# Causal attention pairs on Trainium2: the softmax normalisation moved from VectorE to ScalarE, and two steps of the transposes exchanged

## The reference, cut to what matters

```python
s = jnp.einsum('bqhd,bkhd->bhqk', q_blk, k) * scale     # (+ cumulative forget terms in FoX)
s = jnp.where(k_pos[None, :] <= q_pos[:, None], s, NEG_INF)
p = jax.nn.softmax(s, axis=-1)
return jnp.einsum('bhqk,bkhd->bqhd', p, v)
```

## Time and profile before

| | us |
|---|---|
| median of 3 runs | 1988.62 |
| the runs | 1988.26, 1993.39, 1988.62 |
| profiled execution | 1987.94 |
| its span, first to last instruction | 1986.1 |

### The profile page before, as it was taken

One profiled execution on the slowest core, in us unless ns is written; L12 is line 12 of the kernel. 1 busy time (PEld: TensorE's weight loads), 2 busy tenths in 40 slices (PEclk: granted clock), 3 DMA queues, 4 the chain that ended last, 5 costly groups with the idle time before them and its releaser, 6 DMA issues.

```text
span 1986.1 us, 23674 instructions
## 1 busy us (share of the span) xinstructions
PE 1797.5 (91%) x9188; PEld 1421.2 (72%) x9188; DVE 842.9 (42%) x1805; ACT 761.6 (38%) x1536; POOL 596.5 (30%) x291
## 2 busy tenths in 40 slices
PE   7998998999899999989998979976878999999978
PEld 6676676787688777766666758765756888788766
DVE  1556626586524544254656362576434111000042
ACT  3445543455234434434455433223334232212241
POOL 4222223321343222333212212322102444444422
PEclk9999998999999999989999987887998999999989
DMA  5211233232442221432111324212112333233311
GB/s 145 59 38 41 64 128 111 65 79 50 150 128 75 62 65 54 138 92 59 42 41 54 114 68 108 64 53 64 43 47 65 93 95 105 85 96 95 111 59 64
DMA packets 215578, 157.19 MB, mean 79 GB/s; under 512 B 54635, under 2 KB 197771, under 8 KB 215468
## 3 DMA queue, kind: packets, MB, share of 16 engines
q1 hardware_dynamic: 205120, 128.37, 23.1%
q10 hardware_dynamic: 10044, 27.03, 4.6%
q0 software_dynamic: 304, 0.29, 0.1%
HBM read 146.49 MB, written 9.04 MB: 78 GB/s over the span
## 4 chain that ended last, share of the span: by engine, by line
PE 61%; DVE 11%; ACT 4%; issue 2%; ACTq 2%; POOL 1%; DMA 1%; POOLq 0%; DVEq 0%
PE banks L457 18%; PE banks L459 17%; PE banks L458 16%; PE banks L645 3%; PE banks L615 2%; PE banks L660 2%; POOL w_lo L2300 1%; DVE AB L1875 1%; PE banks L629 1%; DVE AB L1970 1%; DVE AB L1968 1%; ACT w_hi L1115 1%; ACTq L1601 1%; DVE AB L1961 1%; DVE misc L2177 1%
## 5 line engine op out<-in xcount | busy, mean ns | idle before, releaser
L2300 POOL TENSOR_TENSOR w_lo<-w_raw,w_hi 128x1024 fp32r<-128x1024 f32 (+4 forms) x255 | 584.2, 2297 | 1359.1 <-ACT w_hi L1115 1359.0
L457 PE MATMUL banks<-XTh,w_hi 128*128 128x512 f32 (+2 forms) x1080 | 437.3, 405 | 20.2 <-DVE XTl L1918 6.2
L458 PE MATMUL banks<-XTl,w_hi 128*128 128x512 f32 (+2 forms) x1080 | 428.7, 397 | 0.0
L459 PE MATMUL banks<-XTh,w_lo 128*128 128x512 f32 (+2 forms) x1080 | 427.8, 396 | 0.0
L1115 ACT ACTIVATE w_hi<-w_raw 128x1024 fp32r<-128x1024 f32 (+4 forms) x255 | 253.2, 1002 | 223.2 <-PE banks L459 136.9
L457 PEld LDWEIGHTS banks<-XTh,w_hi 128*128 128x128 f32 (+1 forms) x1080 | 209.1, 194 | 71.4 <-issue 19.9
L458 PEld LDWEIGHTS banks<-XTl,w_hi 128*128 128x128 f32 (+1 forms) x1080 | 209.2, 194 | 43.6 <-issue 1.5
L459 PEld LDWEIGHTS banks<-XTh,w_lo 128*128 128x128 f32 (+1 forms) x1080 | 208.2, 193 | 44.9
L1875 DVE TENSOR_SCALAR AB<-AB,ri 128x256 f32<-128x256 f32 (+3 forms) x256 | 186.4, 791 | 2.3
L457 PE MATMUL banks<-w_hi,OTh 128*128 128x512 f32 (+1 forms) x448 | 171.5, 383 | 9.6 <-POOL w_lo L2300 4.2
L459 PE MATMUL banks<-w_hi,OTl 128*128 128x512 f32 (+1 forms) x448 | 167.9, 375 | 0.0
(11 more groups left out here) (200 smaller groups left out, 2511.7 us busy)
## 6 DMA issues: line engine op xcount, KB each, us to landing
w_raw<-in_w_gate_up_dram SPq DMA_DIRECT2D x44, 512.0 KB, 3.8
w_raw<-in_fox_w_in_dram SPq DMA_DIRECT2D x30, 512.0 KB, 4.0
w_raw<-in_mla_w_in_dram SPq DMA_DIRECT2D x26, 512.0 KB, 4.0
w_raw<-in_w_in_dram SPq DMA_DIRECT2D x24, 512.0 KB, 3.7
w_raw<-in_w_down_dram SPq DMA_DIRECT2D x22, 512.0 KB, 3.5
w_raw<-in_swa_w_in_dram SPq DMA_DIRECT2D x20, 512.0 KB, 3.8
w_raw<-in_mla_w_out_dram SPq DMA_DIRECT2D x16, 512.0 KB, 3.5
x_spill<-AB ACTq DMA_DIRECT2D x12, 512.0 KB, 2.6
```

Of the source, the lines that this page charges most:

```text
L457: nc.tensor.matmul(o, ah, bh, start=first, stop=False, skip_group_check=True)
L458: nc.tensor.matmul(o, ah, bl, start=False, stop=False, skip_group_check=True)
L459: return nc.tensor.matmul(o, al, bh, start=False, stop=last, skip_group_check=True)
L2300: pool.tensor_tensor(view(w_lo, u, RING), view(w_raw, u, RAW), view(w_hi, u, RING).bitcast(F32), ALU.subtract).then_inc(lo_done, 1)
```

## The change

In causal pairs DVE makes only the reciprocals (new semaphore `pinv`) and ACT multiplies the rows; in window pairs DVE goes on multiplying, in a form that also writes an accumulator into an unused tile. PE's steps 4 and 5 are exchanged. In `scores`, the plain products of all tiles of a chunk come first, then the rope or forget ones, and only the first tile's first product has the start flag.

```diff
+                    for t in pr.s_chunks[ch]:
+                        ts, ks, cols = at(t)
                         for n, (qp, kp) in enumerate(((QKh, QKh), (QKh, QKl), (QKl, QKh))):
...
-                                                      start=n == 0, stop=n == 2 and not pr.rope and not pr.aug, skip_group_check=True)
+                                                      start=n == 0 and t == pr.s_chunks[ch][0],
+                                                      stop=n == 2 and not pr.rope and not pr.aug, skip_group_check=True)
+                    for t in pr.s_chunks[ch]:
+                        ts, ks, cols = at(t)
                         if pr.aug:
...
                     elif n == 4:
+                        turn(i, 1, 0)
+                    elif n == 5:
                         scores(i + 2, 1)
-                    elif n == 5:
-                        turn(i, 1, 0)
...
+                def norm(i, x):
+                    if not 0 <= i < n_pairs or pairs[i].window:
+                        return
+                    pr, b = pairs[i], (a0 + i) % 2
+                    c.inv += 1
+                    act.wait_ge(pinv, c.inv)
+                    for t in range(T):
+                        sc = pr.score(b, x, t)
+                        ins = nc.scalar.activation(sc, sc, ACT.Copy, scale=ri[:, b, 4 * x + t:4 * x + t + 1])
+                    ins.then_inc(pnorm, 1)
...
                     exps(i + 1, 1)
+                    norm(i + 1, 0)
                     fill(i, 1)
+                    norm(i + 1, 1)
                     fill(i, 2)
...
+                    if not pr.window:
+                        nc.vector.reciprocal(ri[:, b, ns], rs[:, b, ns]).then_inc(pinv, 1)
+                        return
                     link(nc.vector.reciprocal(ri[:, b, ns], rs[:, b, ns]))
                     for t in range(T):
                         ins = nc.vector.tensor_scalar(pr.score(b, x, t), pr.score(b, x, t), ri[:, b, 4 * x + t:4 * x + t + 1],
-                                                      None, ALU.mult)
+                                                      None, ALU.mult, ALU.add, accum_out=unused[:, t:t + 1])
                     ins.then_inc(pnorm, 1)
```

More of the change, by code:

```diff
@@ L226, in build @@
         bf = sb("bf", [P, HEADS])
+        unused = sb("unused", [P, T])
         st = sb("st", [P, 2, 6])
@@ L302, in build @@
         ps_done, ps_free = sem("ps_done"), sem("ps_free")
-        pnb, pexp, pnorm = sem("pnb"), sem("pexp"), sem("pnorm")
+        pnb, pexp, pinv, pnorm = sem("pnb"), sem("pexp"), sem("pinv"), sem("pnorm")
         pt_done, pt_free = sem("pt_done"), sem("pt_free")
@@ L326, in __init__ @@
                 self.cp = self.sq = self.vec = self.idx = self.aug = self.sg = 0
-                self.pair = self.sch = self.tch = self.spill = self.back = 0
+                self.pair = self.sch = self.tch = self.spill = self.back = self.inv = 0
                 self.early = False
@@ L607, in scores, with at @@
                         pe.wait_ge(ps_free, c.sch - 1)
+                    def at(t):
+                        return (slice(t * P, (t + 1) * P), slice((t + 1) * P - pr.keys[t], (t + 1) * P),
+                                slice(pr.s_col(t), pr.s_col(t) + pr.keys[t]))
                     for t in pr.s_chunks[ch]:
-                        ts = slice(t * P, (t + 1) * P)
-                        ks = slice((t + 1) * P - pr.keys[t], (t + 1) * P)
-                        cols = slice(pr.s_col(t), pr.s_col(t) + pr.keys[t])
+                        ts, ks, cols = at(t)
                         for n, (qp, kp) in enumerate(((QKh, QKh), (QKh, QKl), (QKl, QKh))):
@@ L622, in scores @@
                                                       start=False, stop=True, skip_group_check=True)
[L623 to L630, removed]
+                        if pr.rope:
+                            rq, rk, r0 = pr.rope
+                            for n, (qp, kp) in enumerate(((QKh, QKh), (QKh, QKl), (QKl, QKh))):
+                                for x in range(2):
+                                    r = slice(HD * x + r0, HD * x + r0 + ROPE)
+                                    mm = nc.tensor.matmul(bank[2 * (c.sch % 2) + x][:, cols], qp[r, rq, ts], kp[r, rk, ks],
+                                                          start=False, stop=n == 2, skip_group_check=True)
                     mm.then_inc(ps_done, 1)
```

## The result

| | before | after |
|---|---|---|
| median, us | 1988.62 | 2000.67 |
| lowest to highest of five runs | 1985.85 to 1993.39 | 1997.53 to 2005.51 |
| ratio of the times, 95% interval | | 1.006 (1.0039 to 1.008) |
| profiled execution / its span | 1987.94 / 1986.1 | 2005.51 / 2003.7 |

The account below looks back on a forecast made before the run. It took TensorE, busy 91% of the span, as the bound. Terms of +0.35 us at full clock and 3.4 of clock gave +3.8 on the profiled 1987.94, and 0.7 to the median: 1992.4, rounded 1992; range 1980 to 2002.

Parts of the forecast that it names:

- Price of a norm on ACT: Causal pairs: ACT's four row-scaling copies were to take 1.91 us a head, between bounds of 1.43 and 2.28.
- Even pair: MLA, gate then query: PE stalls 1.1 us for query and 0.5 for the next turn's first copy; net +1.15 us.
- Odd pair: MLA, four projections: the 2.9 us rope wait goes; PE waits 2.4 us for query's bank, 1.9 before mix.
- i = 4: MLA: an even fill without a heavy odd one behind it, +1.15 us in each of two stages, +2.3.
- i = 6: MLA: this turn's copies, already holding PE 1.39 us, come behind two norms; +0.6 us in each stage, +1.2.
- FoX i = 5: FoX, only the gate in fill 1: Tanh comes behind two norms and PE waits for the gate's bank, +1.95 us.
- The clock: MLA: the new 2.4 and 1.9 us waits bring half clock with one-half weight; four stretches of 1.7 us, 3.4.
- Rival 2: ScalarE sets the pace of MLA: 2.28 us a head, every half-clock stretch returns, 2004 us; chance 0.18.
- Grouping: Score products: plain ones ahead of rope/aug ones and changed start flags leave the same instructions and operands; no effect.
- Exchange in SWA: PE's new step order: five window pairs wait 0.3 us for ACT's copy, +1.5; the loop's end saves 0.5.
- Accumulator form in SWA: Window pairs: DVE's multiplication takes 0.42 us at 256 columns whatever POOL does; no term for PE's time.
- Rival 1: ACT has room enough: a norm costs 1.43 us a head, the kernel gets faster, 1980 us; chance 0.19.

Follow-up runs that it names:

- e3: The kernel before, with VectorE still normalising all rows but in the accumulator-writing form everywhere; 1973.14 us, ratio 0.9928.
- e4: The kernel before with only the score products grouped (plain ones first) and the start flags changed; 1977.45 us, ratio 0.9951.
- e11: The changed kernel with the old grouping of score products and old start flags; 2008.73 us, ratio 1.0104 to the kernel before.
- e7: The changed kernel with both norms one place later in ACT's queue, behind fill 1 and fill 2; 1956.61 us, ratio 0.9836 to the kernel before.
- e5: The kernel before with VectorE's accumulator form everywhere, grouped score products, and PE's steps 4 and 5 exchanged in causal pairs only; 1958.86 us, ratio 0.9847.

## Why the prediction was right or wrong, step by step

The time, 1992, was 8.7 us short and the measured 2000.7 lies within the range, near its upper end; "within 0.3%" was named likeliest, and it is 0.6% slower. That it came so near is in good part luck: the clock loss was set far too low, and a saving that the forecast did not have hid about half of the error.

- **Price of a norm on ACT, 1.91 us.** Right: 1.92 at 186.31. By groups, ACT in the MLA loop, beside the earlier trace rows:

```profile
L1266 ACT ACTIVATE AB<-AB,ri 128x512 f32<-128x512 f32 x12 | 8.5, 709 | 0.0
L1266 ACT ACTIVATE AB<-AB,ri 128x384 f32<-128x384 f32 x12 | 7.2, 603 | 0.0
L1266 ACT ACTIVATE AB<-AB,ri 128x128 f32<-128x128 f32 x12 | 4.8, 397 | 5.5 <-DVE ri L1892 5.5
L1120 ACT ACTIVATE w_hi<-w_raw 128x384 fp32r<-128x384 f32 x3 | 1.5, 511 | 0.0
```

  The copy with a row operand takes what the exponential takes. The last line is a copy of 384 columns with a constant scale: 92 ns less, which agrees with the 93 ns that the Trainium skill, "ScalarE: Activation LUTs", section "What ACT_TABLE_LOAD costs", gives for the operand.
- **Even pair, stalls of 1.1 and 0.5 us.** Measured 0.87 and 1.01. **Odd pair, 2.4 and 1.9.** Measured 2.51 and 1.51, with the releaser named. The wait for the rope product went, as predicted. **i = 4:** 0.91 and 0.97, the same pair of waits. **i = 6, +0.6:**'s 1.39 became 2.35, +0.96. **FoX i = 5, 1.95:** 2.38 (791.17 to 793.55). Where I replayed the queues, the replay was good to half a microsecond. It does not hold for every pair: in the other three odd pairs the two waits are 1.82 and 0.36, 1.71 and 1.30, 1.71 and 1.51 us.
- **Idle time as a whole.** The sum's terms without the clock add up to +0.40 (the forecast wrote +0.35); with the 6.8 us of old half-clock loss taken as gone in them they mean +7.2 of idle time. Measured +7.6, though not place by place (MLA +3.6 against 6.4, and +1.6 outside the attention stages).
- **The clock: the size that failed.** The forecast ended with 6.8 us of half clock in MLA, 3.4 us of loss. It is 47.8 us, 23.9 of loss. I asked only whether the *long* waits (2.4 and 1.9 us) bring half clock. After the four odd pairs that have them stand 6.8, 3.4, 3.4 us and nothing, 13.6 where the forecast had 6.8. Another 6.8 stands in the first fill; e3, which has no norm on ACT, has it too (98.94 to 105.77), so it can't be laid on the norms. The rest, 27.2 us, follows the two short waits of about 1 us each around a short chunk of scores, and these had been given no clock at all. Rival 2 came nearest: it had every half-clock stretch back, and 2004. Its ground, a dearer norm, was not what happened.
- **Grouping, "the same instructions with the same operands; nothing".** Wrong: -11 us alone (e4), -8 in the changed kernel (e11). The forecast's clock is -6.8 + 3.4 = -3.4 us against before, measured is +20.5 in the profiled pair and about +11 over all executions: 24 or 14 us too little. Grouping hid 8 to 11 of them, and by that the forecast came as near as it did.
- **Exchange in SWA, +1.5 - 0.5.** +3.3 to +3.5: the wait of 0.24 was right, the other 0.37 us a pair, by my reading two more changes between kinds of matmul, was missing.
- **Accumulator form in SWA, nothing for PE.** Right: e3's window loop is 132.2 us against 132.05. On DVE the 256-column multiplication went from 659 to 475 ns.
- **Rival 1's sign of life**, ACT has room enough, was true of ACT's sum and false of its order; with another order (e7) even more than its gain is there.
- **Signs named beforehand.** ACT is busy for 91.0 us from 140 to 281 (93 forecast), L1875 is gone from MLA and FoX, the waits for L1716 of query and keys are there. One sign of rival 2, more half clock, was there too; the other, waits over 20 us in the MLA loop, was not.

## What to carry to other kernels

When work moves to an idle engine, ask where in its queue it goes: one place later, behind the projection copies that TensorE waits for, it cost nothing against VectorE here (e7 1956.6, e5 1958.9); in front of them the same instructions made the kernel 44 us slower. Two short waits of PE around a short group of matmuls cost more in granted clock here than one long wait, so don't price a wait by its length alone. Read the clock from several executions before you put a number on it. Instructions with the same operands have another cost in another order: matmuls of one row count belong together.

## What the runs showed of the hardware

- Two waits of 0.6 to 1.1 us each, with under 3 us of short matmuls between, were followed by PE at 1.2 GHz in 21 of 24 places, in 19 of them for 6.8 us; filling the two waits with matmuls made the kernel 8 us faster. Why 3 of the 24 stayed at 2.4 GHz is open.
- A change of row count between matmuls (64 to 32 or back) cost PE 0.19 us on the mean, and going from 64-row score products to transposes and back up to 0.37 us, what one comparison of two traces leaves over; a two-tile chunk in FoX, with 4 rows as its second kind, fell by 0.4 us too (1.84 to 1.44).
- The accumulator form of the row multiplication took 743 ns on the mean at 128x512 and never over 745 with POOL at work, where the plain form took 1384 on the mean; at 384 columns the plain form was the shorter, 477 against 609 ns.
